# A transformer block with routed experts: joined end, router and corner transfers, fillers on TensorE, four narrow experts last

## The reference

```python
y_a = spatial_gating(u, v, ...) @ w_pa           # gelu, layernorm, mixing over tokens in 8 groups
# bidirectional gated delta rule, 8 heads, chunks, with T = inverse of (I + M) of each chunk
v_new = u_n - w_n @ s;  o_n = qd_n @ s + a_n @ v_new;  s = s * gt_n + kd_n^T v_new
y_b = gdn_output(o_gdn, z, b_norm_g) @ w_pb
x_l = x_l + g1_l * ((sigmoid(gate_a) * y_a + sigmoid(gate_b) * y_b) @ w_out)
h = rmsnorm(x_l, norm2_g) * (1 + sc2) + sh2
scores = sigmoid(h @ w_router)                    # 16 experts in 4 groups; best group, top 2 of it
for e in range(16):
    y = y + combine[:, e:e + 1] * ((silu(h @ w1[e]) * (h @ w3[e])) @ w2[e])
out = rmsnorm(x_l + g2_l * y, final_g)
```

## Time and profile before

| | |
|---|---|
| median of 3 runs | 894.23 us (892.73 to 895.08) |
| the profiled execution | 892.19 us |
| its span | 890.5 us |
| TensorE busy | 779.6 us, 88% |
| VectorE / ScalarE / POOL busy | 525.3 / 428.5 / 209.4 us |
| read from HBM | 190.64 MB |
| TensorE's mean granted clock | 0.959 |

### The profile page before, as it was taken

How to read it: one execution, slowest core, us unless ns; L and a number is a source line. 1 busy time by engine, 2 the same in 40 slices (tenths; PEclk the granted TensorE clock), 3 DMA queues, 4 the chain that set the end, 5 groups by cost and what they waited for, 6 DMA issues and landing times. The chain is left out here.

```text
span 890.5 us, 16008 instructions
## 1 busy us (share of the span) xinstructions
PE 779.6 (88%) x6416; PEld 640.8 (72%) x6416; DVE 525.3 (59%) x778; ACT 428.5 (48%) x758; POOL 209.4 (24%) x367
## 2 busy tenths in 40 slices
PE   3998998999989998899769998967999989899980
PEld 1678876899758996699769778856776666577750
DVE  2497576357753586545564447658884265357725
ACT  2575653448434474345832335454664356336531
POOL 3103170103701136112330102011612122212212
PEclk9999999999999999999988999987999999989995
DMA  9968369436693356934866558862799999999954
GB/s 313 298 217 231 106 167 202 126 83 152 153 225 93 94 148 167 233 81 117 272 140 171 160 150 264 330 259 95 294 351 418 419 421 420 419 400 410 420 215 144
DMA packets 182678, 208.80 MB, mean 234 GB/s; under 512 B 50702, under 2 KB 155831, under 8 KB 169673
## 3 DMA queue, kind: packets, MB, share of 16 engines
q1 hardware_dynamic: 180249, 203.54, 70.2%
q0 software_dynamic: 2352, 4.20, 1.3%
HBM read 190.64 MB, written 21.27 MB: 238 GB/s over the span
## 5 line engine op out<-in xcount | busy, mean ns | idle before, releaser
L2413 PE MATMUL bank<-hT,half_hi 128*128 128x256 f32 (+1 forms) x1024 | 227.9, 318 | 4.0 <-ACT z_raw L1243 2.3
L2413 PEld LDWEIGHTS bank<-hT,half_hi 128*128 128x128 f32 x1024 | 166.0, 191 | 18.6 <-issue 2.9
L2413 PE MATMUL bank<-hT,half_lo 128*128 128x256 f32 (+1 forms) x512 | 159.0, 311 | 0.0
L1699 DVE TENSOR_TENSOR half_lo<-half_raw,half_hi 128x1024 fp32r<-128x1024 f32 x88 | 108.7, 1237 | 40.7 <-ACT half_hi L1127 40.3
L2145 DVE TENSOR_TENSOR w_lo<-raw,w_hi 128x2048 fp32r<-128x2048 f32 x36 | 85.4, 2381 | 71.7 <-ACT w_hi L1568 71.7
L2413 PE MATMUL bank<-lane 64*64 64x64 f32 (+2 forms) x2096 | 101.2, 235 | 16.7 <-issue 6.4
L2413 PEld LDWEIGHTS bank<-lane 64*64 64x64 f32 (+2 forms) x2096 | 92.7, 147 | 29.5 <-issue 18.2
L1127 ACT CAST half_hi<-half_raw 128x1024 fp32r<-128x1024 f32 x88 | 91.9, 1047 | 31.8 <-PE bank L2413 20.7
L2413 PEld LDWEIGHTS bank<-hT,half_lo 128*128 128x128 f32 x512 | 97.5, 190 | 5.5
L1568 ACT CAST w_hi<-raw 128x2048 fp32r<-128x2048 f32 x36 | 68.7, 1908 | 42.2 <-DMA raw<-in_w_e_dram 24.8
L1795 DVE SCALAR_TENSOR_TENSOR chan<-bank,conv_col,chan 128x508 f32<-128x508 f32 (+3 forms) x96 | 63.1, 658 | 6.7 <-ACT chan L1196 4.2
(11 more groups left out here) (362 smaller groups left out, 1375.4 us busy)
## 6 DMA issues: line engine op xcount, KB each, us to landing
raw<-in_w_e_dram SPq DMA_DIRECT2D x96, 1024.0 KB, 11.0
half_raw<-in_w_in_dram SPq DMA_DIRECT2D x64, 512.0 KB, 5.0
half_raw<-in_w_ada_dram SPq DMA_DIRECT2D x32, 512.0 KB, 4.7
raw<-in_w_ada_dram SPq DMA_DIRECT2D x8, 1024.0 KB, 11.3
dense<-staged SPq DMA_DIRECT2D x32, 128.0 KB, 4.5
half_raw<-in_w_proj_a_dram SPq DMA_DIRECT2D x8, 512.0 KB, 5.3
half_raw<-in_w_proj_b_dram SPq DMA_DIRECT2D x8, 512.0 KB, 5.0
half_raw<-in_w_out_dram SPq DMA_DIRECT2D x8, 512.0 KB, 7.1
```

The lines of the kernel that those rows point to most:

```text
L1699: dve.tensor_tensor(half_lo[m % HBUF][:, :], half_raw[n % HRING][:, :], half_hi[m % HBUF][:, :].bitcast(F32), ALU.subtract).then_inc(s["ha ...
L2413: return nc.tensor.matmul(dst, lhsT, rhs, start=start, stop=stop)
```

## The change

1. `FIRST_TURN`, `WIDTH`: four narrow experts come last, ahead of them wide, wide, narrow three times and three wide ones; as many wide ones (9) as before. `narrow_window` moves to `pick`'s place.
2. The last four experts aren't stored or gathered. VectorE multiplies their result by the gate's vector (`late_product`), TensorE adds them to the tokens by one-hot weights (`turn_late`, `add_late`), and four additions from PSUM close. The other rows are gathered after expert 11's store, weighed in expert 14 and summed in expert 15.
3. `move_inverse` has 4 transfers in place of 8, with the same bytes and runs.
4. Several semaphores are shared with earlier loads (router, gates, v and u), with counts to match.
5. In each round `taps(3)` goes ahead of `normed(1, 1)` and `channels(4, 0)` ahead of `turn_back(1, 1)`; in the last pair `scores(3)` and `dense(25)` go ahead of `turn_mix`, and `mix_copies` behind `intra_exp(3)`.
6. Around the routing TensorE gets products of no use (`pass_time`), ScalarE an early Exp of one element, and VectorE does the low gathers first, `rank_loads` after them and `order_experts` within expert 0. `place_rows` gets shorter.

The core of the diff:

```diff
-FIRST_TURN = LISTED + 64
+FIRST_TURN = LISTED
+LATE = 4
...
-WIDTH = [WIDE, WIDE] + 6 * [NARROW, WIDE] + [WIDE, NARROW]
+WIDTH = 3 * [WIDE, WIDE, NARROW] + [WIDE, WIDE, WIDE] + LATE * [NARROW]
...
-                for at_, (to, source) in enumerate(((u_half, u_dram), (t_half, t_dram))):
-                    for d in range(DIRS):
-                        for b in range(2):
-                            load(to[64 * b:64 * b + 64, :, d, :], corner(source, d, b), landed_inverse[at_])
+                for at_, (to, source) in enumerate(((u_by_lane, u_dram), (t_by_lane, t_dram))):
+                    for b in range(2):
+                        load(to[64 * b:64 * b + 64, :, :, :].rearrange("p d m n -> p (d m) n"), corner(source, b), landed_inverse[at_])
...
-            sp.wait_ge(s["y_copied"], 2 * EXPERTS)
-            for nh in range(2):
-                sp.dma_start(y_dram[LISTED:FIRST_TURN, nh * N:nh * N + N], y_out[1][NARROW * nh:NARROW * nh + NARROW, 0:N])\
-                    .then_inc(s["stored"], 16)
...
-            for q in range(EXPERTS - 1):
+            for q in range(STORED):
...
             pool.wait_ge(s["rows_placed"], 1)
-            pool.wait_ge(y_stored[0], 16 * (EXPERTS // 2))
-            pool.wait_ge(y_stored[1], 16 * (EXPERTS // 2 - 1))
+            pool.wait_ge(y_stored[0], 16 * (STORED - STORED // 2))
+            pool.wait_ge(y_stored[1], 16 * (STORED // 2))
             for t in range(2):
                 token_rows(0, t, 0, LISTED).then_inc(s["first_rows"], 16)
-            pool.wait_ge(s["stored"], 32)
             for t in range(2):
-                token_rows(1, t, 0, FIRST_TURN).then_inc(second_rows[t], 16)
+                token_rows(1, t, 0, LISTED).then_inc(second_rows[t], 16)
+            for q in range(STORED + 3, EXPERTS):
+                take_window(q)
             pool.wait_ge(s["overflow_ready"], 1)
...
-            mix_copies()
             decay_exp(3)
             ahead(DENSE_AT[25])
             intra_exp(2)
             dense_copy(25)
             intra_exp(3)
+            mix_copies()
             dense_copy(26)
...
+            act.activation(score[0:1, 0, 0:1], ident[0:1, 0:1], ACT.Exp, scale=-1.0)
...
                     narrow_copy(q - 1)
                 for n in up[3:]:
                     expert_high(n)
-            narrow_copy(EXPERTS - 1)
+                if q == STORED + 1:
+                    act.wait_ge(s["late_turned"], 1)
+                    act.copy(late_rows[:, 0:4, :].rearrange("p k n -> p (k n)"), bank[3][:, :]).then_inc(s["late_copied"], 1)
+                    act.copy(late_rows[:, 4:2 * LATE, :].rearrange("p k n -> p (k n)"), bank[7][:, 0:(2 * LATE - 4) * P]).then_inc(s["late_copied"], 1)
...
+                taps(3)
                 normed(1, 1)
-                taps(3)
...
-            rank_loads()
             gather_low(0)
-            expert_low(2)
             gather_low(3)
             gather_low(6)
-            order_experts()
+            expert_low(2)
+            rank_loads()
...
+            def pick_late():
+                late_of = [P, LATE, 2, RANKED]
+                holds = holder[:, RANKED - LATE:RANKED, :].unsqueeze(2).to_broadcast(late_of)
+                for n, source in enumerate((place, choice)):
+                    own.mark(dve.tensor_tensor(late_found[:, n, :, :, :], source[:, :, FIXED:].unsqueeze(1).to_broadcast(late_of),
+                                               holds, ALU.mult))
+                own.settle()
+                own.after(dve.tensor_reduce(late_at.rearrange("p n j t -> p (n j t)"), late_found.rearrange("p n j t r -> p (n j t) r"),
+                                            AX, ALU.add))
+                own.after(dve.tensor_tensor(late_at[:, 0, :, :], late_at[:, 0, :, :],
+                                            ordered[:, 2, STORED:EXPERTS].unsqueeze(2).to_broadcast([P, LATE, 2]), ALU.subtract))
+                for j in range(LATE):
+                    for t in range(2):
+                        own.mark(dve.tensor_scalar(late_pick[:, j, t, :], slot_iota[:, 0:NARROW], late_at[:, 0, j, t:t + 1],
+                                                   late_at[:, 1, j, t:t + 1], ALU.is_equal, ALU.mult))
+                own.settle()
+                own.mark(dve.tensor_copy(gain_half[0:NARROW, :], ada_vec[0:NARROW, 3, 0:N]))
+                dve.tensor_copy(gain_half[NARROW:P, :], ada_vec[NARROW:P, 3, N:2 * N]).then_inc(s["rows_placed"], 1)
+            def late_product(q):
+                dve.wait_ge(s["unit_used"], DOWN_FIRST[q] + 2)
+                dve.wait_ge(y_stored[q % 2], 16 * ((STORED + 1 - q % 2) // 2))
+                dve.tensor_tensor(late_out(q), work_bank(q, 2)[:, :], gain_half[:, :], ALU.mult).then_inc(s["late_ready"], 1)
+            def weigh(n, t):
+                return dve.scalar_tensor_tensor(out=y_tok[:, n, t, :], in0=y_tok[:, n, t, :], scalar=pair_weight[:, n, t:t + 1],
+                                                in1=ada_vec[:, 3, :], op0=ALU.mult, op1=ALU.mult)
+            def weigh_rows():
+                dve.wait_ge(s["first_rows"], 32)
+                for t in range(2):
+                    own.mark(weigh(0, t))
+                for t in range(2):
+                    dve.wait_ge(second_rows[t], 16)
+                    own.mark(weigh(1, t))
+            def sum_rows():
+                own.settle()
+                own.after(dve.tensor_tensor(y_tok[:, 0, :, :], y_tok[:, 0, :, :], y_tok[:, 1, :, :], ALU.add))
+                own.after(dve.tensor_tensor(y_tok[:, 0, :, :], y_tok[:, 0, :, :], x_lat, ALU.add))
...
+                if q == 0:
+                    order_experts()
                 if q == 1:
                     place_rows()
+                if q == STORED:
+                    pick_late()
+                if q == EXPERTS - 1:
+                    sum_rows()
+                if q > STORED:
+                    late_product(q - 1)
+                if q == EXPERTS - 2:
+                    weigh_rows()
             narrow_act(EXPERTS - 1)
+            late_product(EXPERTS - 1)
             def expert_turn(i):
                 dve.tensor_copy(turn_int[0:1, :], first_int[0:1, 1, bass.ds(i * 2, 2)]).then_inc(s["offsets_ready"], 1)
...
-            own.mark(weigh(0, 0))
-            own.after(weigh(0, 1))
-            own.mark(dve.tensor_tensor(x_lat, x_lat, y_tok[:, 0, :, :], ALU.add))
...
             for t in range(2):
-                dve.wait_ge(second_rows[t], 16)
-                own.after(weigh(1, t))
-                dve.tensor_tensor(x_lat[:, t, :], x_lat[:, t, :], y_tok[:, 1, t, :], ALU.add).then_inc(s["x2_ready"], 1)
+                dve.wait_ge(s["late_sum"], t + 1)
+                for nh in range(2):
+                    ins = dve.tensor_tensor(x_lat[:, t, nh * N:nh * N + N], y_tok[:, 0, t, nh * N:nh * N + N],
+                                            bank[LATE_BANK[2 * t + nh]][:, :], ALU.add)
+                ins.then_inc(s["x2_ready"], 1)
...
+            def pass_time(n, into):
+                for _ in range(n):
+                    mm(into[:, 0:P], ident[:, :], ident[:, :])
...
+                channels(4, 0)
                 turn_back(1, 1)
-                channels(4, 0)
...
             scores(2)
-            turn_mix()
             scores(3)
             dense(25)
+            turn_mix()
...
             project_out(1, 3)
+            pass_time(8, bank[7])
             turn_x_again(1, 0)
+            pass_time(2, bank[7])
             logits(1, 0)
             turn_x_again(1, 1)
+            pass_time(2, bank[7])
             logits(1, 1)
+            pass_time(18, bank[7])
...
+            pass_time(16, bank[7])
...
+            def turn_late():
+                pe.wait_ge(s["rows_placed"], 2)
+                pe.wait_ge(s["y_copied"], 2 * STORED)
+                for k in range(2 * LATE):
+                    into = bank[3][:, k * P:(k + 1) * P] if k < 4 else bank[7][:, (k - 4) * P:(k - 3) * P]
+                    for half in range(2):
+                        ins = mm(into[NARROW * half:NARROW * half + NARROW, :], late_pick[:, k // 2, k % 2, :], ident[:, :])
+                ins.then_inc(s["late_turned"], 1)
+            def add_late(j):
+                pe.wait_ge(s["late_ready"], j + 1)
+                pe.wait_ge(s["act_split"], EXPERTS - 1)
+                pe.wait_ge(s["late_copied"], 2)
+                for t in range(2):
+                    for nh in range(2):
+                        rows_ = slice(NARROW * nh, NARROW * nh + NARROW)
+                        ins = mm(bank[LATE_BANK[2 * t + nh]][:, :], late_rows[rows_, 2 * j + t, :], late_out(STORED + j)[rows_, :],
+                                 j == 0, j == LATE - 1)
+                    if j == LATE - 1:
+                        ins.then_inc(s["late_sum"], 1)
             for q in range(EXPERTS):
                 up = up_half if WIDTH[q] == WIDE else narrow_up
                 up(q, 0)
                 if q:
                     turn_of(q - 1)
                 up(q, 1)
```

(7 more changed lines are left out.)

139 lines of the change are left out of this document (82 added, 57 removed).

## The result

The changed kernel takes **885.33 us** (median of six runs, 882.84 to 888.78) where the kernel before took 895.17 in the same session: ratio 0.9886, 95% interval 0.9854 to 0.9918, 9.8 us faster. The forecast was 871.2. The profiled execution took 885.05 us around a span of 883.4 (before 890.5), mean granted clock 0.983.

A forecast was written before the change was run, and what follows sets the result against it. Bounds: TensorE's gaps ahead of the routing, the experts' weight stream, and the chain after TensorE's last product. Terms -13.2 - 4.8 + 5.0 - 0.35 - 3.0 - 3.0 - 3.6 = -23.0 us gave 871.2 us, range 862 to 881.

The forecast's parts named there:

- The end: After TensorE's last down product: 12.0 us left in place of 25.2, as most rows are gathered and weighed earlier; -13.2 us.
- Pairs: Three rounds ahead of the last pair: earlier keys and joined corners, 1.0 us each round, -3.0 us (0 to -7).
- the bound "nothing": Pairs: one end of the range for the joined corners, no gain because the DMA engines are full with short packets.
- a rival for the narrow run: Last four narrow experts: granted clock stays at 0.50 behind DMA waits, +29 us on the forecast, 900 us; chance 0.03.
- The joined corners' part: Corner transfers, 8 issues become 4 with the same bytes: between nothing and about 2 us gained a round.
- Last pair: Fourth score to corners: exponent 2.8 us earlier without the mixing work ahead, 1.0 for corners, 0.2 off for hand-overs; -3.6 us.
- Routing: Fillers keep the clock up at the gather products and low copies come sooner: -3.0 us for the stream, bounds -1 and -5.
- The stream: Expert weight stream: four gathers, 2.1 MB, move into it, +5.0 us; fewer stored rows, -0.35 us.
- Which seven slots absorb: Weight stream: three wide experts in a row lose 4.9 us of TensorE time, which seven weight slots take up.
- the first rival: Corners and stream don't move (joined corners, start eaten by `rank_loads`, or stream starved by three wide experts): 878 us; chance 0.16.
- The last experts: With four narrow experts last, TensorE takes down units as they land; last down product ends 860.5 against 865.3, -4.8 us.
- signs named: Wrong if: DMA below 9 after 650 us, low clock past 800, VectorE awaiting gathers past 845, keys wait gone without longer corner wait.

## Why the prediction was wrong

**The end** (-13.2): right, -13.3; from the last down product 11.9 us against 12.0.

**Pairs** (-3.0): wrong, with the wrong sign. The step that failed is "I take 1.0 each, nearer to the full engines: -3.0 us (0 to -7)". That time won at the keys is lost at the corners was right, but the bound "nothing" was taken for the worst case. The idle time moved to the corners, from a place with slack to one without. The order alone costs 3.1 us in the old kernel, and its undoing wins 4 in the new one: that is shown. That it costs them by the clock, which fell behind the longer waits, is what the profiles say, all of the loss being behind the first 64x64 products. The prediction priced a low clock as a rival for the narrow run and for the routing, never for a wait that its own change made longer. The row was there: the second round's wait for the corners was 2.34 us, and what was won at the keys had to come on top (3.31 in the kernel after; the first round's went from 0.64 to 2.63). The joined corners' part is 0, as by the Trainium skill (DMA: Bandwidth & Descriptors, Anatomy of one DMA), whose rule I set against my 1.0. That section is on transfers issued by GpSimd, and these are SP's, but the trace agrees with it: the time isn't in the issue. A transfer of 256 KB took 7.1 us from issue to landing, the halves 5.3 and 4.3, while an issue took 1.2 us.

**Last pair** (-3.6): the fourth exponent did come earlier, by 2.9 us against the rest of the pair:

```profile
432.10 1.15 ACT L1274 ACTIVATE lane<-bank,gates 128x128 f32<-128x128 f32 x4
...
434.03 5.64 SPq L605 DMA_DIRECT2D problem_rows<-lane  x4
```

(before 428.44, when the pair had started 6.55 us earlier). The step that failed is the next link, "rows moved at 431.43", which was to come 2.8 us sooner. SP issues the rows of the first three tiles before the fourth's, and these two issues ended only at 437.9; the fourth tile was ready at 435.1. In the kernel before they had ended at 430.23:

```profile
427.48 2.75 SPq L587 DMA_DIRECT2D problem_rows<-lane  x1
...
431.43 1.05 SPq L587 DMA_DIRECT2D problem_rows<-lane  x1
```

So SP's queue stood idle for the fourth tile for 1.2 us, and the rest of the wait that I removed had been hidden behind the first two issues. Even the 1.2 us didn't come through, as these two ended 1.1 us later against the start of the pair: the third issue comes 11.4 us behind that start in both kernels.

**Routing** (-3.0): right in size. TensorE gained 4.8 us, and the stream 3.8. Slots are freed by VectorE's low copies, and those of the first expert started at 613.12 and 619.08 us (before 609.16 and 614.85), since the low gathers stand ahead of the second; SP's next two loads went out at 615.43 and 621.39, 4.0 and 4.2 us later than before, though TensorE was only 0.9 late. But from the eleventh load on the gain is there. The fifth and the thirteenth load of expert weights, before and then after:

```profile
588.15 0.33 SPq L587 DMA_DIRECT2D raw<-in_w_e_dram  x1
...
632.12 0.33 SPq L587 DMA_DIRECT2D raw<-in_w_e_dram  x1
```

```profile
593.40 0.33 SPq L605 DMA_DIRECT2D raw<-in_w_e_dram  x1
...
633.55 0.33 SPq L605 DMA_DIRECT2D raw<-in_w_e_dram  x1
```

5.3 us late ahead of the routing, 1.4 behind it, and 1.5 at the twenty-seventh. The other ten profiles with the change's routing fillers show the same, 3.7 to 3.9 us; the one without them shows none of it (592.73 and 636.75, 4.6 us late at both). About 1 us of it is lost again by the thinner stretch from 650 to 660 us, since the loads land 2.4 us late behind it.

**The stream** (+4.65): the gathers were right in bytes. From 650 us to the end of the stream 87.6 MB were moved against 85.5, 2.2 MB or 5.2 us at 420 GB/s; the rest, some 3 us, is the two stretches that are thinner than before, 650 to 660 us (291 against 362 GB/s) and 800 to 820 us (366 against 397). "Which seven slots absorb" is the step that failed for the second: the three wide experts did starve the stream, as the first rival had it, but by 1.5 us. Against the loads' 2.4 us behind the routing the end of the stream, at 8.3, is 5.9 us later where 4.65 were forecast.

**The last experts** (-4.8): I had all additions but `add_late(2)` in the slack of the stream. The first two experts' 3.70 us stand behind the last up product, where the wait for the next weights was 0.64 us. Without them the last down product ends 4.0 us behind the stream in place of 8.7, which is the -4.8; with them 6.6.

So of the 16 us that this profile is short of the forecast (the medians 13) 2.8 are chance, 6.8 are the rounds, 2.7 the last pair, 2.7 the last experts, and the routing and the stream together 1.0. Of the rivals the first (878 us) was the nearest. Of its mechanisms the joined corners gave nothing, as it said, and the stream was starved by 1.5 us, but the start of the experts wasn't eaten. The measured 885 lay above the range because the rounds, the last pair and the last experts failed together, and the first of them had a bound only on the good side. Of the signs named, two came true, DMA below 9 tenths between 650 and 660 us (a share of 0.82) and VectorE waiting for a gather until 851.63 us; VectorE's next work but one, at 853.37, waited for TensorE and not for the gather, so that wait cost nothing that the trace shows.

## What to carry to other kernels

When a wait is taken from TensorE, ask where the same idle time turns up next, and whether the products behind that place have slack; a wait ahead of slack is the cheaper one. To price an earlier step follow it to the first queue that issues in order: the step gains no more than that queue stood idle for it, here 1.2 us at most in place of 2.8. To see whether a gain reaches a stream, follow more than its next two transfers. And extra work "in the slack of the stream" has to be placed product by product between two waits for weights.

## What the runs showed of the hardware

**The start.** The five late starts (2.4 to 3.1 us behind the kernel before) come with slower products on TensorE. The same eight products, in the timeline of the kernel before and then of the kernel after:

```profile
26.17 1.05 PE L2413 MATMUL bank<-fold,lane 128*128 128x2 f32 x8 [0.70 <-ACT lane L1135]
```

```profile
26.25 1.87 PE L2479 MATMUL bank<-fold,lane 128*128 128x2 f32 x8 [0.70 <-ACT lane L1150]
```

They took 1.05 us in the nine early profiles and 1.87 in the five late ones, and products of 512 columns, 0.39 us otherwise, take up to 0.63 until about 33 us, though the granted clock of both stretches reads 1.00 and the DMA rows are alike (347 GB/s in both). So here the duration of a known product shows a slow stretch that the granted clock's column doesn't; no run shows what sets it.

**The clock behind the corners.** In all nine profiles with the new keys' order it was 0.77 to 0.90 over the 15 us behind the corners of the first and of the second round; with the old order it was 1.00 in four, and 1.00 and 0.90 in the kernel before. The same 64 products took 3.68 us behind a wait of 5.33, and 2.08 where fillers had left a wait of 1.43.
